# First mixing stage: the steps of the head pairs from the first scores on come half an input unit later

## The chip, the core and the metric

The kernel runs on one core of a Trainium2 chip. A core has several engines that each work through a list of instructions of their own, in order: TensorE (PE in the profile) multiplies matrices and transposes 128x128 tiles, VectorE (DVE) and ScalarE (ACT) work on rows of elements, GpSimd (POOL) does a little elementwise work, and SyncE (SP) issues most transfers from memory. The engines meet through semaphores: an instruction may wait until a counter that others raise has reached a value, and whatever stands behind it in its engine's list waits too. The metric is the device time of one execution in microseconds (us); the median of the runs is compared.

## What is computed

Two blocks of a transformer-like network on 256 positions of 1024 features, all in float32: four feed-forward parts with three mixing parts between them. The change touches only the first mixing part. In the reference it is this:

```python
h = rmsnorm(x, mix_pre_g);  q, k, v, qb, kb, vb = split(h @ w_qkv)
a = gqa_dense(axial_rope(norm(q)), axial_rope(norm(k)), v)    # 8 heads of 64, 2 key/value heads
b = dilated_mixture(rope(qb), rope(kb), vb)                   # 8 heads of 64, windowed patterns
x = x + rmsnorm(concat(a, b) @ w_out, mix_post_g)
```

Each head computes scores q k^T, the exponentials of the scores less the row's maximum, divides by the row's sum, and multiplies with the values. The three dilated patterns of the second kind are folded into one table that is added to the scores.

## The kernel before

To keep float32 accuracy every weight matrix is split in two parts, a rounded "high" and the rest, "low"; each product is made of three passes (`PASSES`). Weights arrive by SyncE in items of 128x2048 numbers (`gu_raw`, two slots). ScalarE writes the high part (`gu_high`, line 1168), VectorE the low part (`gu_low`, line 1808), and only then may TensorE use the item (it waits for `gu_split`). An item's slot may be overwritten by ScalarE when TensorE has finished the item two before it (`wait_used`).

In the first mixing stage (span time 200 to 301 us) TensorE first makes the four pair units 0 to 3, then the input units 4 to 8, each with `project` (line 670: 48 matmuls, 24 for each half, `halves`), and last the output units (`out_unit`, line 793). Between the input units stand the steps of the eight head pairs (`PAIRS`), each a chain that goes from engine to engine:

- TensorE `pair_scores(p)` (line 746) into banks 4 and 5; it waits until the exponentials of pair p-1 are done (`p_ready`, pairs 1 to 4), or its maxima (`max_ready`, from pair 5 on)
- VectorE `pair_max(p)` (lines 2194 and 2197, from pair 4 on 2203 and 2208)
- ScalarE `pair_exps(p)` (line 1494)
- VectorE `pair_normal(p)` (lines 2214 and 2216)
- TensorE `pair_transposes(p)` (line 759), ScalarE `pair_pT_out(p)` (line 1505)
- TensorE `pair_values(p)` (line 777) into one bank, number 3, for pairs 0 to 6. It waits for `o_ready` of the pair before, that is, until ScalarE's `pair_high` (line 1510) and VectorE's `pair_low` (line 2222) have both read that bank.

Beside them run the rotary steps of the queries and keys: `rope_raw` (line 1448) and `rope_in_out` (line 1435) on ScalarE, `rope_turn` (line 2173) and `rope_sum` (line 2182) on VectorE, products on GpSimd (line 2602), `rope_transposes` (line 731) on TensorE. `values_in` (line 1481) takes values out of PSUM.

Nothing sorts this work: the order on each engine is the order in which the calls are written, in three lists by hand, one each for TensorE, ScalarE and VectorE. `next_high(v)` and `next_low(v)` split item v+2 of the stage, in the middle of these lists; `out_high(0, u)` and `out_low(0, u)` split item 11+u.

Short names below: P5a is the first half of input unit 5, P5b the second; S, T and V with a pair's number are the scores, transposes and values of TensorE; M, E and N are a pair's maxima (VectorE), exponentials (ScalarE) and division (VectorE). "Item 8" is the stage's item 8, which input unit 8 uses.

Of the kernel before, what the change touches and what calls it, by code (L numbers as in the profile page):

```python
# [148 lines left out]
def build(nc, a):  # L149
    with ExitStack() as ctx:  # L150
# [245 lines left out]
        def rope_heads(r):  # L396


            return 2 if r == 2 else 4
# [108 lines left out]
        def _(pe):  # L508
# [145 lines left out]
            def project(m, v, feature, halves=range(2)):  # L654

                item = MIX_ITEM[m] + v
                sl = item % 2
                pe.wait_ge(s["gu_split"], item + 1)
                if (m, v) in ((0, 4), (0, 5)):
                    wait_unit(pe, 0, "pair 0")  # L660
                elif v >= 2:
                    wait_unit(pe, m, 0 if v < 4 else v - 2)
                for h in halves:
                    for k in range(KC):
                        for pw_, px in PASSES:
                            wk = gu[pw_][:, sl, k * SEQ:(k + 1) * SEQ]
                            cut_ = slice(h * P, (h + 1) * P)
                            lhsT, rhs = ((wk[:, cut_], hT[px][:, k, :]) if feature
                                         else (hT[px][:, k, cut_], wk))
                            i = nc.tensor.matmul(unit_bank(v)[:, h * SEQ:(h + 1) * SEQ], lhsT, rhs,  # L670
                                                 start=(pw_, px, k) == (0, 0, 0),
                                                 stop=(pw_, px, k) == (1, 0, KC - 1))
                if h == 1:
                    i.then_inc(s["proj_done"], 1)
# [48 lines left out]
            def rope_transposes(k):  # L723

                pe.wait_ge(s["rop_ready"], k + 1)
                if k:
                    pe.wait_ge(s["ropT_evac"], k)
                w = rope_heads(ROPES[k]) * HD
                for c in range(w // P):
                    for t in range(TT):  # L730
                        i = nc.tensor.transpose(bank(2)[:, c * SEQ + t * P:c * SEQ + (t + 1) * P],
                                                rop[:, k % 2, t * w + c * P:t * w + (c + 1) * P], ident[:, :])
                i.then_inc(s["ropT_psum"], 1)

            def pair_scores(p):


                pe.wait_ge(s["ropT_evac"], (2, 2, 3, 3, 5, 5, 7, 7)[p])
                if p:
                    pe.wait_ge(s["p_ready" if p <= PAIRS // 2 else "max_ready"], p)  # L740
                c = p % 4
                for t in range(TT):
                    for e in range(2):
                        half = slice(64 * e, 64 * e + 64)
                        q, k = (qT[0], kTA[half, :]) if p < PAIRS // 2 else (qT[1], kTB[half, c, :])
                        i = nc.tensor.matmul(bank(4 + e)[:, t * SEQ:(t + 1) * SEQ],
                                             q[half, c, t * P:(t + 1) * P], k, start=True, stop=True)
                i.then_inc(s["s_ready"], 1)

            def pair_transposes(p):  # L750

                pe.wait_ge(s["pn_ready"], p + 1)
                if p:
                    pe.wait_ge(s["pt_ready"], p)
                for e in range(2):
                    for kt in range(TT):
                        for t in range(TT):
                            o, f = kt * SEQ + t * P, 2 * SEQ * e + t * SEQ + kt * P
                            i = nc.tensor.transpose(bank(6 + e)[:, o:o + P], pair_probs[:, p % 2, f:f + P],
                                                    ident[:, :])  # L760
                i.then_inc(s["pt_psum"], 1)
# [104 lines left out]
            pair_unit(1, 1, 1, range(4, 8))  # L866
            project(0, 4, False)
            rope_transposes(1)
            pair_scores(0)
            project(0, 5, False)  # L870
            rope_transposes(2)
            pair_scores(1)
            pair_transposes(0)
            project(0, 6, False, (0,))
            rope_transposes(3)
            pair_scores(2)
            pair_values(0)
            pair_transposes(1)
            project(0, 6, False, (1,))
            rope_transposes(4)  # L880
            pair_scores(3)
            pair_values(1)
            pair_transposes(2)
            project(0, 7, False, (0,))
            pair_scores(4)
            pair_values(2)
            pair_transposes(3)
            rope_transposes(5)
            project(0, 7, False, (1,))
            pair_scores(5)  # L890
            pair_values(3)
            pair_transposes(4)
            project(0, 8, False, (0,))
            rope_transposes(6)
            pair_values(4)
            pair_scores(6)
            pair_transposes(5)
            project(0, 8, False, (1,))
            pair_scores(7)
            pair_values(5)  # L900
            pair_transposes(6)
            def pair_out(k):

                return s["o_ready"], k + 1

            wait_unit(pe, 0, 8)
            out_unit(0, 0, 0, range(4), pair_out)
            pe.wait_ge(s["ropT_evac"], 7)
            out_unit(0, 0, 1, range(4), pair_out)
            pair_transposes(7)  # L910
            pair_values(6)
            for t in range(TT):
                out_unit(0, 1, t, (4, 5), pair_out)
            pair_values(7)
# [219 lines left out]
        def _(act):  # L1134
# [304 lines left out]
            def rope_raw(k):  # L1439

                v, r = ROPE_AT[k], ROPES[k]
                if k >= 2:
                    act.wait_ge(s["rop_ready"], k - 1)
                act.wait_ge(s["proj_done"], v + 1)
                w = rope_heads(r) * HD
                src = unit_bank(v).rearrange("p (t n) -> p t n", t=TT)
                for t in range(TT):
                    i = nc.scalar.activation(raw[:, k % 2, t * w:(t + 1) * w], src[:, t, 0:w], ACT.Copy,
                                             scale=st["rinv"][:, t:t + 1])
                i.then_inc(s["raw_ready"], 1)  # L1450
# [61 lines left out]
            def next_high(v):  # L1512

                gu_high(MIX_ITEM[0] + v + 2)
# [18 lines left out]
            step.mark(nc.scalar.activation(st["warm"][:, 0:1], col(COL_HALFPI), ACT.Exp))  # L1533
            step.done(act)
            next_high(4)
            pair_exps(0)
            rope_raw(4)
            values_in(5)
            rope_in_out(2)
            pair_exps(1)  # L1540
            pair_pT_out(0)
            rope_in_out(3)
            next_high(5)
            pair_high(0)
            pair_exps(2)
            pair_pT_out(1)
            rope_raw(5)
            next_high(6)
            rope_in_out(4)
            pair_high(1)  # L1550
            pair_exps(3)
            pair_pT_out(2)
            pair_high(2)
            pair_exps(4)
            pair_pT_out(3)
            rope_in_out(5)
            rope_raw(6)
            next_high(7)
            pair_high(3)
            pair_exps(5)  # L1560
            pair_pT_out(4)
            rope_in_out(6)
            pair_high(4)
            pair_exps(6)
            pair_pT_out(5)
            values_in(8)
            next_high(8)
            pair_high(5)
            pair_exps(7)
            pair_pT_out(6)  # L1570
            pair_pT_out(7)
            out_high(0, 0)
# [229 lines left out]
        def _(dve):  # L1802
# [382 lines left out]
            def next_low(v):  # L2185

                gu_low(MIX_ITEM[0] + v + 2)
# [46 lines left out]
            rope_squares(2)  # L2234
            next_low(3)
            rope_turn(2)
            pair_max(0)
            rope_sum(2)
            rope_turn(3)
            next_low(4)  # L2240
            pair_normal(0)
            pair_max(1)
            rope_sum(3)
            rope_turn(4)
            pair_normal(1)
            rope_sum(4)
            pair_max(2)
            next_low(5)
            pair_low(0)
            pair_normal(2)  # L2250
            pair_max(3)
            next_low(6)
            pair_low(1)
            rope_turn(5)
            rope_sum(5)
            pair_normal(3)
            pair_max(4)
            pair_low(2)
            pair_normal(4)
            pair_max(5)  # L2260
            rope_turn(6)
            rope_sum(6)
            pair_low(3)
            pair_normal(5)
            pair_max(6)
            pair_low(4)
            next_low(7)
            pair_normal(6)
            pair_max(7)
            pair_low(5)  # L2270
            pair_normal(7)
            next_low(8)
            pair_low(6)
            out_low(0, 0)
            pair_low(7)
# [588 lines left out]
```

## Time and profile before

| | us |
|---|---|
| median of 3 runs | 1085.87 (1085.01 to 1086.59) |
| span of the profiled execution | 1083.0 |
| TensorE busy in it | 1067.1 (99%) |
| VectorE busy | 790.6 (73%) |
| ScalarE busy | 589.8 (54%) |
| GpSimd busy | 215.0 (20%) |

The span goes from the first to the last instruction of one profiled execution; 1085.87 - 1083.0 = 2.9 us lie around it. A timeline row is read so: start, duration, engine, line, operation, what it writes and reads, and in brackets how long the engine had been idle before it and who ended that. The recorded duration of an instruction runs some 0.1 us into the start of the next on the same engine, so a step's cost in a row of steps is the distance between starts.

### The profile page before, as it was taken

How to read it: one execution, taken by the hardware profiler on the slowest of the kernel's cores; microseconds unless marked ns; L12 is line 12 of the kernel's file. 1: busy time of each engine (PE TensorE's matmuls, PEld its weight loads, DVE VectorE, ACT ScalarE, POOL GpSimd, SP SyncE). 2: the span in 40 equal slices, each digit the busy share in tenths (PEclk: the TensorE clock that was granted, in tenths of full speed). 3: DMA queues.
4: the chain of work that ended last, by engine and by line, in shares of the span. 5: the costliest groups of instructions: out<-in, count | busy, mean ns of one | idle time of the engine just before them, and what ended most of it. 6: DMA issues, size and time to landing. Idle time of an engine off the chain costs nothing.

```text
span 1083.0 us, 18769 instructions
## 1 busy us (share of the span) xinstructions
PE 1067.1 (99%) x7028; PEld 939.0 (87%) x7028; DVE 790.6 (73%) x1092; ACT 589.8 (54%) x853; POOL 215.0 (20%) x224
## 2 busy tenths in 40 slices
PE   9999999999999999999999999999999999999997
PEld 8888889888788888898998988888899888888886
DVE  5867776897678888766776788777559557777674
ACT  6546444767766445455785644554443565544453
POOL 0006000031069997000000398000000000000001
PEclk9999999999999999999999999999999999999999
DMA  7775455332445656552434754645434235645541
GB/s 260 294 245 203 177 177 206 128 150 79 146 163 187 217 179 228 181 210 95 147 126 156 247 199 175 232 175 177 172 125 161 98 126 183 225 175 181 207 154 39
DMA packets 37025, 189.64 MB, mean 175 GB/s; under 512 B 3824, under 2 KB 4592, under 8 KB 22640
## 3 DMA queue, kind: packets, MB, share of 16 engines
q1 hardware_dynamic: 34528, 181.22, 46.4%
q10 hardware_dynamic: 2160, 6.70, 1.9%
q0 software_dynamic: 288, 1.05, 0.3%
q8 instruction: 33, 0.54, 0.2%
q14 instruction: 16, 0.13, 0.0%
HBM read 187.90 MB, written 1.05 MB: 174 GB/s over the span
## 4 chain that ended last, share of the span: by engine, by line
PE 86%; DVE 6%; ACT 4%; issue 2%; DMA 1%; SPq 0%; DVEq 0%; ACTq 0%
PE ps L558 23%; PE ps L629 19%; PE ps L563 12%; PE ps L670 8%; PE ps L793 6%; PE ps L570 6%; PE ps L590 1%; DMA gu_raw<-in_wgu 1%; DVE gu_low L1808 1%; PE ps L692 1%; PE ps L605 1%; ACT gu_high L1168 1%; PE ps L518 1%; PE ps L710 1%; PE ps L617 1%
## 5 line engine op out<-in xcount | busy, mean ns | idle before, releaser
L558 PE MATMUL ps<-hT,gu_high 128*128 128x512 f32 x1152 | 286.8, 391 | 0.0
L558 PEld LDWEIGHTS ps<-hT,gu_high 128*128 128x128 f32 x1152 | 211.5, 188 | 41.6 <-DVE gu_low L1943 0.4
L1943 DVE TENSOR_TENSOR gu_low<-gu_raw,gu_high 128x2048 fp32r<-128x2048 f32 x83 | 196.0, 2361 | 7.4 <-ACT gu_high L1293 4.3
L563 PEld LDWEIGHTS ps<-hT,gu_low 128*128 128x128 f32 x1152 | 157.2, 190 | 11.2
L1293 ACT ACTIVATE gu_high<-gu_raw 128x2048 fp32r<-128x2048 f32 x84 | 160.4, 1909 | 9.1 <-PE ps L570 8.3
L563 PE MATMUL ps<-hT,gu_low 128*128 128x256 f32 x1152 | 160.6, 282 | 0.0
L1269 ACT ACTIVATE ffn_s<-ffn_s 128x256 f32<-128x256 f32 x88 | 36.8, 418 | 178.5 <-DVE ffn_s L1910 143.4
L1947 DVE TENSOR_TENSOR dn_low<-dn_raw,dn_high 128x1024 fp32r<-128x1024 f32 x84 | 112.1, 1334 | 2.7 <-ACT dn_high L1301 2.7
L1925 DVE TENSOR_TENSOR ffn_s<-ps,ffn_s 128x256 f32<-128x256 f32 x72 | 30.6, 425 | 109.2 <-ACT ffn_s L1281 109.2
L1301 ACT ACTIVATE dn_high<-dn_raw 128x1024 fp32r<-128x1024 f32 x84 | 88.7, 1056 | 35.8 <-PE ps L629 35.8
L1168 ACT ACTIVATE gu_high<-gu_raw 128x2048 fp32r<-128x2048 f32 x37 | 70.8, 1914 | 68.5 <-PE ps L670 35.1
L1808 DVE TENSOR_TENSOR gu_low<-gu_raw,gu_high 128x2048 fp32r<-128x2048 f32 x35 | 81.1, 2318 | 35.8 <-ACT gu_high L1168 35.8
L629 PE MATMUL ps<-dn_high,act_high 128*128 128x512 f32 x320 | 100.2, 394 | 1.2 <-DVE act_low L1935 0.7
L629 PE MATMUL ps<-dn_low,act_high 128*128 128x512 f32 x320 | 99.1, 391 | 0.0
L629 PE MATMUL ps<-dn_high,act_low 128*128 128x512 f32 x320 | 98.9, 390 | 0.0
L629 PEld LDWEIGHTS ps<-dn_low,act_high 128*128 128x128 f32 x320 | 60.1, 188 | 13.4
L629 PEld LDWEIGHTS ps<-dn_high,act_low 128*128 128x128 f32 x320 | 60.1, 188 | 13.1
L670 PE MATMUL ps<-hT,gu_high 128*128 128x256 f32 x384 | 70.2, 285 | 0.0
L570 PE MATMUL ps<-hT,gu_high 128*128 128x256 f32 x384 | 70.0, 284 | 0.0
L1275 ACT ACTIVATE ffn_s<-ps 128x256 f32<-128x256 f32 x72 | 27.3, 379 | 77.3 <-PE ps L563 77.2
L629 PEld LDWEIGHTS ps<-dn_high,act_high 128*128 128x128 f32 x320 | 54.9, 190 | 9.0 <-issue 2.4
L570 PEld LDWEIGHTS ps<-hT,gu_high 128*128 128x128 f32 x384 | 60.3, 192 | 0.6
(336 smaller groups left out, 1865.1 us busy)
## 6 DMA issues: line engine op xcount, KB each, us to landing
gu_raw<-in_wgu SPq DMA_DIRECT2D x126, 1024.0 KB, 4.8
dn_raw<-in_wdn SPq DMA_DIRECT2D x88, 512.0 KB, 5.3
x<-in_x SPq DMA_DIRECT2D x2, 512.0 KB, 5.6
gu_raw<-in_wgu SPq DMA_DIRECT2D x2, 512.0 KB, 6.5
scratch<-in_glu ACTq DMA_DIRECT2D x1, 1024.0 KB, 10.9
scratch<-in_biasM ACTq DMA_DIRECT2D x1, 1024.0 KB, 6.2
s5in<-in_s5in ACTq DMA_DIRECT2D x1, 768.0 KB, 4.3
out_x<-scratch SPq DMA_DIRECT2D x3, 256.0 KB, 2.4
```

Source lines behind the costliest of these rows:

```text
L558: nc.tensor.matmul(out, gu[0][:, sl, o:o + P], hT_both[:, k, :, :].rearrange("p a s -> p (a s)"), start=k == 0, stop=False)
L563: i = nc.tensor.matmul(out[:, 0:SEQ], gu[1][:, sl, o:o + P], hT[0][:, k, :], start=False, stop=k == KC - 1)
L570: i = nc.tensor.matmul(out[:, 0:SEQ], gu[pw_][:, sl, o:o + P], hT[px][:, k, :], start=(pw_, px, k) == (0, 0, 0), stop=(pw_, px, k) == (1, ...
L629: i = nc.tensor.matmul(bank(2 * t + half), act_s[px][:, h, t * P:(t + 1) * P], dn[pw_][:, h, half * 512:half * 512 + 512], start=start and ...
L670: i = nc.tensor.matmul(unit_bank(v)[:, h * SEQ:(h + 1) * SEQ], lhsT, rhs, start=(pw_, px, k) == (0, 0, 0), stop=(pw_, px, k) == (1, 0, KC ...
L793: i = nc.tensor.matmul(out, oT[px][:, k, t * P:(t + 1) * P], both, start=(pw_, px, k) == (0, 0, own) and j % 2 == 0, stop=(pw_, px, k) == ...
L1168: nc.scalar.activation(gu[0][:, g % 2, :], gu_raw[:, g % 2, :], ACT.Copy) \
L1293: nc.scalar.activation(gu[0][:, sl, :], gu_raw[:, sl, :], ACT.Copy) \
L1301: nc.scalar.activation(dn[0][:, 1 - h, :], dn_raw[:, 1 - h, :], ACT.Copy) \
L1808: nc.vector.tensor_tensor(gu[1][:, g % 2, :], gu_raw[:, g % 2, :], gu[0][:, g % 2, :], ALU.subtract).then_inc(s["gu_split"], 1)
L1943: nc.vector.tensor_tensor(gu[1][:, sl, :], gu_raw[:, sl, :], gu[0][:, sl, :], ALU.subtract).then_inc(s["gu_split"], 1)
L1947: nc.vector.tensor_tensor(dn[1][:, 1 - h, :], dn_raw[:, 1 - h, :], dn[0][:, 1 - h, :], ALU.subtract) \
```

## The change

Each of the three lists is written in another order; no instruction is added or removed. On TensorE the units are cut in halves, and each step of a pair stands half a unit further back in the order of the units: S0 came ahead of P5a and now comes ahead of P5b, and so on. V1 stood before P7a and stands behind it, V6 now comes before T7, and the first output unit's first tile comes before V5. The lists of ScalarE and VectorE follow.

```diff
             rope_transposes(1)
+            project(0, 5, False, (0,))
             pair_scores(0)
-            project(0, 5, False)
+            project(0, 5, False, (1,))
             rope_transposes(2)
             pair_scores(1)
+            project(0, 6, False, (0,))
             pair_transposes(0)
-            project(0, 6, False, (0,))
             rope_transposes(3)
             pair_scores(2)
+            project(0, 6, False, (1,))
             pair_values(0)
             pair_transposes(1)
-            project(0, 6, False, (1,))
             rope_transposes(4)
             pair_scores(3)
+            project(0, 7, False, (0,))
             pair_values(1)
             pair_transposes(2)
-            project(0, 7, False, (0,))
             pair_scores(4)
+            project(0, 7, False, (1,))
...
             out_unit(0, 0, 1, range(4), pair_out)
+            pair_values(6)
             pair_transposes(7)
-            pair_values(6)
...
             next_high(4)
+            rope_raw(4)
             pair_exps(0)
-            rope_raw(4)
             values_in(5)
+            next_high(5)
             rope_in_out(2)
...
+            pair_exps(2)
+            rope_raw(5)
+            pair_pT_out(1)
+            rope_in_out(4)
+            next_high(6)
             pair_high(0)
...
             pair_normal(1)
             rope_sum(4)
             pair_max(2)
-            next_low(5)
+            pair_normal(2)
+            rope_turn(5)
+            next_low(6)
+            rope_sum(5)
             pair_low(0)
-            pair_normal(2)
             pair_max(3)
```

In the changed kernel all lines behind TensorE's list stand one further down (1168 is 1169, and so on).

The first place is ScalarE's list around `pair_high(0)`, which writes `dn_high`. Before, from the split of item 7 (line 1168) on:

```order
L1168 ACTIVATE gu_high<-gu_raw 128x2048
L1510 ACTIVATE dn_high<-ps 128x256
L1494 ACTIVATE scratch,stat<-ps,stat 128x256 x4
L1505 ACTIVATE scratch<-ps 128x1024
L1448 ACTIVATE scratch<-ps,small 128x256 x2
L1168 ACTIVATE gu_high<-gu_raw 128x2048
L1435 ACTIVATE scratch<-ps 128x512
```

and now, from E2 on, with the split of item 8 in line 1169:

```order
L1495 ACTIVATE scratch,stat<-ps,stat 128x256 x4
L1449 ACTIVATE scratch<-ps,small 128x256 x2
L1506 ACTIVATE scratch<-ps 128x1024
L1436 ACTIVATE scratch<-ps 128x512
L1169 ACTIVATE gu_high<-gu_raw 128x2048
L1511 ACTIVATE dn_high<-ps 128x256
L1495 ACTIVATE scratch,stat<-ps,stat 128x256 x4
```

`pair_high(0)` stood ahead of E2, behind the split of item 7; it now stands behind E2, three further steps and the split of item 8.

The second place is VectorE's list around `pair_low(0)`, which writes `dn_low`. Before, from M2 on:

```order
L2194 TENSOR_REDUCE stat<-ps 128x2x2
L2197 TENSOR_SCALAR stat<-stat 128x2x2
L1808 TENSOR_TENSOR gu_low<-gu_raw,gu_high 128x2048
L2222 TENSOR_TENSOR dn_low<-ps,dn_high 128x256
L2214 RECIPROCAL stat<-stat 128x2x2
L2216 TENSOR_TENSOR scratch<-scratch,stat 128x1024
L2194 TENSOR_REDUCE stat<-ps 128x2x2
```

and now, from M2 on:

```order
L2195 TENSOR_REDUCE stat<-ps 128x2x2
L2198 TENSOR_SCALAR stat<-stat 128x2x2
L2215 RECIPROCAL stat<-stat 128x2x2
L2217 TENSOR_TENSOR scratch<-scratch,stat 128x1024
L2174 TENSOR_TENSOR scratch<-scratch 128x512
L1809 TENSOR_TENSOR gu_low<-gu_raw,gu_high 128x2048
L2183 TENSOR_TENSOR scratch<-scratch 128x512
L2223 TENSOR_TENSOR dn_low<-ps,dn_high 128x256
L2195 TENSOR_REDUCE stat<-ps 128x2x2
```

The low part of item 7 between M2 and `pair_low(0)` has moved ahead, and N2, `rope_turn(5)`, the low part of item 8 and `rope_sum(5)` now stand there.

The third place is TensorE's list behind the first output unit (line 793): before

```order
L793 MATMUL ps<-gu_high,dn_low 128x512
L793 MATMUL ps<-gu_low,dn_high 128x512
L759 MATMUL ps<-ident,scratch 128x128 x8
L777 MATMUL ps<-scratch 64x256 x4
L793 MATMUL ps<-gu_high,dn_high 128x512
```

and now

```order
L793 MATMUL ps<-gu_high,dn_low 128x512
L793 MATMUL ps<-gu_low,dn_high 128x512
L777 MATMUL ps<-scratch 64x256 x4
L759 MATMUL ps<-ident,scratch 128x128 x8
L793 MATMUL ps<-gu_high,dn_high 128x512
```

V6 (line 777) has moved from behind T7 (line 759) to ahead of it.

## Rows read from the trace of the kernel before

**Rows 1.** The page, part 1: busy time, share of the span and instructions of each engine.

```profile
PE 1067.1 (99%) x7028; PEld 939.0 (87%) x7028; DVE 790.6 (73%) x1092; ACT 589.8 (54%) x853; POOL 215.0 (20%) x224
```

**Rows 2.** TensorE's timeline, 228 to 238 us: where it stood idle.

```profile
228.08 1.14 PE L746 MATMUL ps<-scratch 64*128 64x256 f32 x8 [0.69 <-ACT scratch L1435]
...
237.15 1.09 PE L759 MATMUL ps<-ident,scratch 128*128 128x128 f32 x8 [0.49 <-DVE scratch L2216]
```

**Rows 3.** The chain that ended last, in order of time, 238 to 244 us.

```profile
238.25 2.87 PE ps L670 x24
241.12 0.44 PE ps L731 x4
241.55 1.06 PE ps L746 x8
242.62 1.01 PE ps L777 x8
243.63 1.02 PE ps L759 x8
```

**Rows 4.** VectorE's timeline: item 5's low part, steps of the pairs, the last `pair_low`.

```profile
225.96 2.28 DVE L1808 TENSOR_TENSOR gu_low<-gu_raw,gu_high 128x2048 fp32r<-128x2048 f32 x1
...
232.60 2.83 DVE L1808 TENSOR_TENSOR gu_low<-gu_raw,gu_high 128x2048 fp32r<-128x2048 f32 x1
...
246.62 0.17 DVE L2214 RECIPROCAL stat<-stat 128x4 f32<-128x4 f32 x1
246.82 1.23 DVE L2216 TENSOR_TENSOR scratch<-scratch,stat 128x1024 f32<-128x1024 f32 x1
249.07 1.23 DVE L2194 TENSOR_REDUCE stat<-ps 128x4 f32<-128x1024 f32 x1 [1.02 <-PE ps L746]
250.33 0.17 DVE L2197 TENSOR_SCALAR stat<-stat 128x4 f32<-128x4 f32 x1
250.40 2.29 DVE L1808 TENSOR_TENSOR gu_low<-gu_raw,gu_high 128x2048 fp32r<-128x2048 f32 x1
252.61 0.42 DVE L2222 TENSOR_TENSOR dn_low<-ps,dn_high 128x256 fp32r<-128x256 f32 x1
...
253.66 0.69 DVE L2182 TENSOR_TENSOR scratch<-scratch 128x512 f32<-128x512 f32 x1
...
287.89 0.42 DVE L2222 TENSOR_TENSOR dn_low<-ps,dn_high 128x256 fp32r<-128x256 f32 x1
```

**Rows 5.** ScalarE's timeline, 247 to 254 us, without its accumulator reads.

```profile
247.62 0.84 ACT L1448 ACTIVATE scratch<-ps,small 128x256 f32<-128x256 f32 x2 [0.56 <-PE ps L670]
248.34 1.91 ACT L1168 ACTIVATE gu_high<-gu_raw 128x2048 fp32r<-128x2048 f32 x1
250.15 0.60 ACT L1435 ACTIVATE scratch<-ps 128x512 f32<-128x512 f32 x1
250.62 0.39 ACT L1510 ACTIVATE dn_high<-ps 128x256 fp32r<-128x256 f32 x1
250.89 0.49 ACT L1494 ACTIVATE scratch<-ps,stat 128x256 f32<-128x256 f32 x1
...
252.68 1.07 ACT L1505 ACTIVATE scratch<-ps 128x1024 f32<-128x1024 f32 x1
```

**Rows 6.** GpSimd's timeline: the rotary products of two steps (x2 each).

```profile
229.16 1.95 POOL L2602 TENSOR_TENSOR scratch<-scratch 128x256 f32<-128x256 f32 x2 [5.61 <-DVE scratch L2162]
232.03 3.98 POOL L2602 TENSOR_TENSOR scratch<-scratch 128x256 f32<-128x256 f32 x2 [0.93 <-DVE scratch L2182]
```

**Rows 7.** The same chain behind T7, 282 to 286 us.

```profile
282.18 1.01 PE ps L777 x8
283.20 2.94 PE ps L793 x12
```

**Rows 8.** Windows at the end of the span: length, busy us (instructions), granted clock, DMA.

```profile
1075.00:1080.00 5.00, 0.56 (x3) 0.13 (x1) 3.55 (x7) 2.69 (x7) 3.25 (x2) 1.00 0.16 61
1080.00:1083.00 3.00, 0.00 (x0) 0.00 (x0) 0.00 (x0) 0.00 (x0) 0.00 (x0) 0.53 0.66 247
```

More of the change, by code:

```diff
@@ L888, in _ @@
             rope_transposes(5)
-            project(0, 7, False, (1,))
             pair_scores(5)
+            project(0, 8, False, (0,))
+            rope_transposes(6)
             pair_values(3)
             pair_transposes(4)
-            project(0, 8, False, (0,))
-            rope_transposes(6)
+            pair_scores(6)
+            project(0, 8, False, (1,))
             pair_values(4)
-            pair_scores(6)
             pair_transposes(5)
-            project(0, 8, False, (1,))
             pair_scores(7)
-            pair_values(5)
-            pair_transposes(6)
             def pair_out(k):
@@ L907, in _ @@
             out_unit(0, 0, 0, range(4), pair_out)
+            pair_values(5)
+            pair_transposes(6)
             pe.wait_ge(s["ropT_evac"], 7)
             out_unit(0, 0, 1, range(4), pair_out)
+            pair_values(6)
             pair_transposes(7)
-            pair_values(6)
             for t in range(TT):
@@ L1542, in _ @@
             rope_in_out(3)
-            next_high(5)
-            pair_high(0)
[L1545 to L1549, printed above, removed]
+            pair_exps(2)
[3 more added lines that the diff above has]
+            next_high(6)
+            pair_high(0)
+            pair_exps(3)
             pair_high(1)
-            pair_exps(3)
             pair_pT_out(2)
+            pair_exps(4)
+            rope_raw(6)
             pair_high(2)
-            pair_exps(4)
             pair_pT_out(3)
             rope_in_out(5)
-            rope_raw(6)
             next_high(7)
+            pair_exps(5)
+            rope_in_out(6)
             pair_high(3)
-            pair_exps(5)
             pair_pT_out(4)
-            rope_in_out(6)
+            pair_exps(6)
+            values_in(8)
             pair_high(4)
-            pair_exps(6)
             pair_pT_out(5)
-            values_in(8)
             next_high(8)
+            pair_exps(7)
             pair_high(5)
-            pair_exps(7)
             pair_pT_out(6)
@@ L2236, in _ @@
             rope_turn(2)
+            rope_sum(2)
             pair_max(0)
-            rope_sum(2)
             rope_turn(3)
@@ L2241, in _ @@
             pair_normal(0)
+            rope_sum(3)
             pair_max(1)
-            rope_sum(3)
             rope_turn(4)
+            next_low(5)
             pair_normal(1)
@@ L2247, in _ @@
             pair_max(2)
-            next_low(5)
+            pair_normal(2)
+            rope_turn(5)
+            next_low(6)
+            rope_sum(5)
             pair_low(0)
-            pair_normal(2)
             pair_max(3)
-            next_low(6)
+            pair_normal(3)
             pair_low(1)
-            rope_turn(5)
-            rope_sum(5)
-            pair_normal(3)
             pair_max(4)
+            pair_normal(4)
+            rope_turn(6)
             pair_low(2)
-            pair_normal(4)
+            rope_sum(6)
             pair_max(5)
-            rope_turn(6)
-            rope_sum(6)
+            next_low(7)
+            pair_normal(5)
             pair_low(3)
-            pair_normal(5)
             pair_max(6)
+            pair_normal(6)
             pair_low(4)
-            next_low(7)
-            pair_normal(6)
             pair_max(7)
+            next_low(8)
+            pair_normal(7)
             pair_low(5)
-            pair_normal(7)
-            next_low(8)
             pair_low(6)
```

## The prediction, made before the changed kernel was run

> **What bounds the kernel now.** I read the page first: TensorE is busy for 99% of the span [rows 1]. A step on another engine costs nothing while TensorE has work, and each microsecond that TensorE stands idle is lost. TensorE's timeline comes next, from the second rotary transpose (227 us) to the last output unit (301 us). It shows two idle pieces: 0.69 us ahead of S0 and 0.49 us ahead of T0 [rows 2]. From there on the chain that ended last is TensorE's own list, step behind step [rows 3]. So the change can win at most 0.69 + 0.49 = 1.2 us, 0.1% of the span, since it takes no instruction away. What it can lose is set by the chains between the engines, which had slack behind 238 us and get another order.
>
> **The prices.** TensorE: a half unit 2.87, rotary transposes 0.44, scores 1.06, values 1.01, transposes 1.02 [rows 3]. VectorE: a low part 2.2 to the next step and 2.3 to its signal (recorded 2.29, with the next step 2.21 behind its start); maxima from 249.07 to 250.33 + 0.17 = 250.50, 1.4; division from 246.62 to 246.82 + 1.23 = 248.05, 1.4; rotary turn or sum 0.6 between starts (recorded 0.69), `pair_low` 0.4 [rows 4]. ScalarE, by distances between starts: `rope_raw` 0.7, a high part 1.8, `rope_in_out` 0.5, `pair_high` 0.3, four exponentials 250.89 to 252.68, 1.8 and 0.1 more to the signal; the copy of the transposes 1.0 [rows 5].
>
> **Wait 1, P5a.** P5a now stands where S0 stood. TensorE is free at 228.08 - 0.69 = 227.4 [rows 2]. S0 waited there for the rotary queries; P5a needs the low part of item 5, which ends at 225.96 + 2.28 = 228.2 [rows 4], and its place in VectorE's list has not moved. P5a starts at 228.3: wait 0.9. The old wait is not taken away; it gets 0.2 longer with another name.
>
> **Wait 2, S1.** S0 starts at 228.3 + 2.87 = 231.2, ends at 232.2. M0 starts at 232.3 and ends at 233.7, E0 ends 1.9 later, 235.7 (the `rope_raw` now ahead of E0 is done by then: GpSimd's products for its slot end at 229.16 + 1.95 = 231.1 [rows 6], the sum 0.7 later, and it takes 0.7 itself). TensorE is ready for S1 at 232.2 + 2.87 + 0.44 = 235.5. Before, the whole of unit 5 stood between S0 and S1; now one half. Wait 0.2, S1 at 235.7.
>
> **Wait 3, S2.** VectorE goes on from M0 at 233.7: turn 0.6, low part of item 6 2.2, N0 1.4, sum 0.6, M1 1.4: 239.9. N0 and the sum now stand ahead of M1. E1 ends at 241.8, S2 can start at 241.9. TensorE: 235.7 + 1.06 + 2.87 + 1.02 + 0.44 = 241.1. Wait 0.8. P6a needs item 6's low part, ready at 236.6, when S1 ends at 236.8: no wait. T0 comes at 239.6, N0 is done at 237.9: the old wait of 0.49 ahead of T0 is gone, covered by P6a.
>
> **Wait 4, V1, the main one.** V1 overwrites bank 3 and needs `pair_low(0)`. The chain to it, from M1's end at 239.9: VectorE turn 0.6, low part of item 7 2.2, N1 1.4, sum 0.6, M2 1.4: 246.1. ScalarE E2 1.9, `rope_raw(5)` 0.7, copy 1.0, `rope_in_out` 0.5, high part of item 8 1.8: 252.0. VectorE can't begin the low part of item 8 before, and behind it stand `rope_sum(5)` and then `pair_low(0)`: 2.2 + 0.6 + 0.4 = 3.2, 255.2. TensorE comes to V1 at 241.9 + 1.06 (S2) + 2.87 (P6b) + 1.01 (V0) + 1.02 (T1) + 0.44 + 1.06 (S3) + 2.87 (P7a) = 252.2. Wait 3.0. `pair_high(0)` needs V0, which is over at 246.8, so it is the order of ScalarE's and VectorE's lists that holds it, not TensorE: it is queued behind E2, three steps and a high part. P7a, now ahead of V1, is no cover for it: it has been counted.
>
> **Wait 5, S4.** M3 stands in VectorE's list behind `pair_low(0)`: 255.2 + 1.4 = 256.6, E3 ends at 258.5. TensorE comes to S4, which needs E3, at 255.2 + 1.01 + 1.02 = 257.2. Wait 1.3.
>
> **Then cover again.** From S4 on each S has at least a half unit and two steps of a pair behind it (2.87 + 1.01 + 1.02 = 4.9 us) while S waits, from S5 on, for the maxima of the pair before alone (1.4 in the dense form; the form with the table has no row here, and even twice that is covered). The other moves of items lie under this and cost 0, as long as that slack of some 2 us holds.
>
> **Wait 6, the last pair.** From T7's end at 282.18 [rows 7] to the end of `pair_low(7)` at 287.89 + 0.42 = 288.31 [rows 4] there are 6.1 us: copy, high part of item 11, `pair_high(6)`, low part of item 11, `pair_low(7)`, none of which moves. Before, TensorE had V6 1.01, four pieces of output 2.94, V7 1.01 and two pieces 2.94 / 2 = 1.47 between [rows 7], 6.4 us, just enough. V6 now stands ahead of T7: 5.4 us are left against 6.1 and the signal. Wait 0.8.
>
> **The sum.** 0.9 + 0.2 + 0.8 + 3.0 + 1.3 + 0.8 = 7.0 us of waits, less the 1.2 us that were there: 5.8 us more. One price is not settled: GpSimd's products of one step took 3.98 us in place of 1.95 [rows 6], and the low part begun beside them 2.83 in place of 2.28 [rows 4]. Now the same products begin with M0, near 232, and the low part of item 6 at 234.3. If they still meet, 0.55 is added to M1 and S2 with it: 6.3. If not, 5.8. I take 6.0, since half of the products' long time reaches past 234.3. Everything behind the stage is relative to TensorE's last output unit and shifts whole: 1083.0 + 6.0 = 1089.0 of span, and with the 2.9 us around it **1091.9**.
>
> The Trainium skill, GPSIMD Engine Reference, section Specifications, says that GpSimd shares its SBUF interfaces with VectorE and that the contention comes with VectorE instructions in a two-port mode or with two SBUF inputs. The maxima read PSUM, so by that rule the products would be over sooner and the sum 5.8; rows 6 and 4 agree with the collision itself, and no row shows the products beside the maxima.
>
> **Rivals.**
> - *The halves do cover.* What the order is for: each chain gets half a unit more, both old waits go, nothing replaces them. 1085.87 - 1.2 = 1084.7, not slower. For it: behind 238 us the old chain has no step of another engine in it, V1 had no wait at all [rows 3]. It decides at V1: the chain from M1 to `pair_low(0)` must be 3 us shorter than its 15.3 us, and M3 with it. Against it: its pieces are queued work with recorded durations, not waits. It could only be if `pair_high(0)` did not stand where the list of ScalarE puts it, which the rows of the order exclude. Chance 0.06, of it 0.02 for faster by over 0.2%.
> - *The chains are a little quicker.* Steps on VectorE and ScalarE run 5% under the rows. Each S-to-S and the V1 chain then shrink, waits 2 and 3 nearly go and wait 4 falls by 0.8: some 3.7 us more, 1089.6. Chance 0.08.
> - *The clock falls.* TensorE stands idle 3.0 us, works 2.0 and stands 1.3. In the old trace the granted clock stays 1.00 through the window with 0.56 us of work in 5 and is 0.53 in the next [rows 8], so the lower level, 1.2 GHz, comes behind an idle stretch longer than this one. If it came here, V1, T2 and P7b (1.01 + 1.02 + 2.87 = 4.9 us) would take up to double: 2 to 5 us on top, 1094 to 1097. Chance 0.08.
> - *More waits in a row.* The slack behind S4 is less than I count and S3, S6 or a T waits too: 7.5 to 8.5 us, up to 1094.4. Chance 0.08.
>
> The Trainium skill, TensorE: Matmul & The Clock Gate, section Why this matters for your kernels, warns of gaps of idle between bursts of matmuls, after which the clock goes back to the half rate. By that rule the third rival would be likelier than I put it; the trace's own long idle stretch, with the clock still full in its first part, speaks for the lower chance.
>
> **How the numbers follow.** Forecast 0.70, rivals 0.06, 0.08, 0.08, 0.08. The range runs from the quick chains (1089.2, a little under 1089.6) to the many waits (1094.5); it leaves out the first rival and the clock. A measurement of this kernel can tell about 0.2% (2.2 us) from no change, so the bounds are 1083.7 and 1088.0: faster 0.02, within 0.05, slower 0.93.
>
> **What would show it.** Right: TensorE's timeline after has an idle piece of some 3 us ahead of V1 (line 778), released by `dn_low`, at 252 us; one of about 1 us ahead of S4, released by exponentials; one under 1 us in the output unit behind V7; no idle piece ahead of T0; and P5a waits for `gu_low` where S0 waited. The first part of the span up to 227 us is as before. Wrong: V1 starts within 0.5 us of P7a's end; or the granted clock is below 1.00 between 250 and 270 us; or the time is lost behind 301 us.

## The result, and the profile after

The changed kernel takes 1094.55 us (median of 4 runs, 1093.11 to 1095.16) against 1086.23 us (4 runs, 1085.01 to 1086.80): a ratio of 1.0080, 95% interval 1.0068 to 1.0092. It is slower, as forecast, by 8.3 us where 6.0 was forecast, and 1094.55 lies 0.05 us above the range's end of 1094.5. A second set of the same two kernels gave 1093.16 against 1085.59, 7.6 us; that time lies inside the range. So on which side of the bound the time falls is scatter; that more than 6.0 us are lost shows in the length of the stage, below.

The profiled execution of the changed kernel has a span of 1092.5 us; its own time was 1094.26, so 1.8 us lie around a span. The page of after, busy time (compare [rows 1]): TensorE does the same work in a longer span.

```profile
PE 1070.8 (98%) x7028; PEld 940.7 (86%) x7028; DVE 790.3 (72%) x1092; ACT 590.3 (54%) x853; POOL 213.8 (20%) x224
```

TensorE's timeline of after, the rows behind an idle stretch in the first mixing stage (start, duration, what; in brackets the idle time before it and who ended it). They answer to [rows 2].

```profile
229.91 0.51 PE L670 MATMUL ps<-gu_high,hT 128*128 128x256 f32 x2 [1.09 <-DVE gu_low L1809]
...
244.04 1.14 PE L746 MATMUL ps<-scratch 64*128 64x256 f32 x8 [0.83 <-ACT scratch L1495]
...
257.32 1.18 PE L777 MATMUL ps<-scratch 128*64 128x256 f32 x8 [2.48 <-DVE dn_low L2223]
...
260.62 1.60 PE L746 MATMUL ps<-scratch 64*128 64x256 f32 x8 [0.22 <-ACT scratch L1495]
...
297.67 0.47 PE L793 MATMUL ps<-gu_high,dn_high 128*128 128x512 f32 x1 [0.90 <-DVE dn_low L2223]
```

There were two idle stretches, 1.2 us in all; now there are five, 5.5 us. In the order of the rows: P5a for item 5's low part; S2 for E1; V1 for `pair_low(0)`; S4 for E3; the output unit for `pair_low(7)`. These are the places that the prediction named, with the releasers that it named, and T0 waits no more.

One number for the stage serves all runs: from the start of the second rotary transposes to the start of the next part's first transposes. Before it is 300.89 - 226.80 = **74.1 us**, after 309.99 - 228.21 = **81.8 us**. So 7.7 us are lost in the stage. TensorE's timeline of after at the two ends:

```profile
228.21 0.60 PE L731 MATMUL ps<-ident,scratch 128*128 128x128 f32 x4
...
309.99 1.16 PE L518 MATMUL ps<-ident,x 128*128 128x128 f32 x8
```

The windows of after, where the stage's clock is not full (length, busy us of TensorE, its weight loads, VectorE, ScalarE, GpSimd, granted clock, DMA share, GB/s):

```profile
256.00:258.00 2.00, 0.68 (x7) 0.57 (x8) 2.00 (x4) 0.00 (x0) 0.00 (x0) 1.00 0.18 25
258.00:260.00 2.00, 2.00 (x12) 1.57 (x8) 0.48 (x2) 1.45 (x7) 0.00 (x0) 0.55 0.93 348
260.00:262.00 2.00, 1.78 (x10) 1.11 (x8) 1.45 (x3) 1.67 (x5) 0.00 (x0) 0.60 0.38 152
262.00:264.00 2.00, 2.00 (x18) 1.85 (x16) 1.90 (x10) 0.04 (x1) 0.00 (x0) 1.00 0.00 0
```

The third rival came too, in small: behind V1's wait the granted clock fell to half, the lower of its two levels (1.2 GHz), for some 3 us. T2 and S4 ran in that stretch; TensorE's timeline shows T2 of after and then T2 of before, the same eight transposes.

```profile
258.43 1.97 PE L759 MATMUL ps<-ident,scratch 128*128 128x128 f32 x8
```

```profile
249.97 1.09 PE L759 MATMUL ps<-ident,scratch 128*128 128x128 f32 x8
```

### The profile page after: what moved, and what is told of

Its sections match the earlier page's. It is cut to its first block, busy times and chain, and to the rows that moved or that the text cites. A ratio compares the mean times of both kernels' runs of the same rounds, so it can differ in the third digit from the quotient of the medians.

```text
span 1092.5 us, 18770 instructions
## 1 busy us (share of the span) xinstructions
PE 1070.8 (98%) x7028; PEld 940.7 (86%) x7028; DVE 790.3 (72%) x1092; ACT 590.3 (54%) x853; POOL 213.8 (20%) x224
## 3 DMA queue, kind: packets, MB, share of 16 engines
q0 software_dynamic: 288, 1.05, 0.3%
HBM read 187.90 MB, written 1.05 MB: 173 GB/s over the span
## 4 chain that ended last, share of the span: by engine, by line
PE 85%; DVE 7%; ACT 4%; issue 2%; DMA 1%; SPq 0%; DVEq 0%; ACTq 0%
PE ps L558 22%; PE ps L629 19%; PE ps L563 12%; PE ps L670 7%; PE ps L570 6%; PE ps L793 6%; PE ps L590 2%; DVE gu_low L1809 2%; DMA gu_raw<-in_wgu 1%; ACT gu_high L1169 1%; PE ps L692 1%; PE ps L518 1%; PE ps L605 1%; PE ps L710 1%; PE ps L617 1%
```

## The experiments

In each the stage's length is what is compared. It was 81.8 and 81.7 us in two profiles of the changed kernel, though single waits ahead of an edit also moved by up to 0.25 us from one profile to the next; the time of a run repeats only within 1 to 2 us. "Price" below is the distance between the starts of two neighbours in TensorE's list.

**1. The changed kernel again (e1_again).**

> The changed kernel once more. Measure of all runs: the stage's length on TensorE, from the start of the second rotary transposes (line 731 or 732, behind unit 4) to the start of the next part's first transposes (line 518); before 300.89 - 226.80 = 74.1 us, changed 309.99 - 228.21 = 81.8 us. Theory (all of the loss is in the stage): 81.8 within 0.3 again, with the clock at half speed for some 3 us behind V1's wait; the 1.4 us by which the changed kernel's profile was later already at the stage's start is scatter of the start, and is another number here. Rival: that offset comes with the change; then it is 1.4 again.

Measured: stage 81.7, time 1.0065 times before (1.0048 to 1.0082), the same waits to 0.01 us (V1 2.49, S2 0.83, the output unit 0.90), clock at half speed again from 257 to 260 us. Its stage starts at 227.0 instead of 228.2. The loss of 7.6 to 7.7 us is the stage's; the 1.4 us by which after's profile was late at the stage's start is scatter.

**2. `pair_low(0)` alone ahead of item 8's split (e2_low0).** On ScalarE and VectorE:

```diff
             pair_exps(2)
+            pair_high(0)
             rope_raw(5)
             pair_pT_out(1)
             rope_in_out(4)
             next_high(6)
-            pair_high(0)
...
             pair_normal(2)
+            pair_low(0)
             rope_turn(5)
             next_low(6)
             rope_sum(5)
-            pair_low(0)
             pair_max(3)
```

> Changed kernel, pair_high(0) straight behind E2 and pair_low(0) straight behind N2, ahead of the split of item 8. Theory (queues): V1's wait of 2.5 us goes, but M3 is still behind the low part of item 8 and rope_sum(5), so E3 ends near 260 and the wait moves to S4, some 3.4 us instead of 0.2 and the slow T2; stage 80.5 to 81.3. Rival (V1's bank is the loss): stage 78.7 or less, S4 waits under 1.5 us.

Measured: stage 82.8; ratio 1.0082 (1.0057 to 1.0107). V1 starts 3.07 us after P7a, with no wait; the wait is at S4. TensorE's timeline of this run:

```profile
258.65 2.08 PE L746 MATMUL ps<-scratch 64*128 64x256 f32 x8 [3.68 <-ACT scratch L1495]
```

3.68 us of idle where 3.4 were expected, and not a microsecond won: M3 is still queued behind the low part of item 8, and S4 needs M3. What was not expected is 1.5 us more on top: the granted clock is at half for some 3 us as in after, but here that stretch falls on S4, which takes 2.0 instead of 1.06, and on the next half unit, which takes 3.68 instead of 3.07. Here nothing covers it.

```profile
258.00:260.00 2.00, 1.35 (x6) 1.32 (x8) 1.43 (x3) 1.69 (x5) 0.00 (x0) 0.67 0.56 225
260.00:262.00 2.00, 2.00 (x10) 1.35 (x8) 1.54 (x8) 0.00 (x0) 0.00 (x0) 0.50 0.00 0
```

(Windows of this run, columns as above.)

**3. M3 too ahead of item 8's split (e3_low0_max3).** As 2, and on VectorE `pair_max(3)` behind `pair_low(0)`, ahead of `rope_turn(5)`.

> As e2_low0, and M3 too stands ahead of the low part of item 8. Theory (queues): V1 and S4 wait for nothing, the clock stays at 1.00: 2.6 (V1) + 1.3 (T2 and S4's wait) + 0.5 (S4 at half clock) less, stage 77.4 within 0.4, about 4.3 us under the changed kernel. Rival: another late step takes their place, stage over 79.

Measured: stage 78.2; time 1.0028 times before (1.0018 to 1.0038), 1089.3 us. Neither V1 nor S4 waits, the clock is 1.00. 3.6 us are won where 4.3 were expected, and 78.2 lies outside the expected 77.4 within 0.4; the difference is a wait that was hidden behind the others, S6 for the rotary keys' copy, in TensorE's timeline of this run:

```profile
269.96 1.13 PE L746 MATMUL ps<-scratch 64*128 64x256 f32 x8 [0.60 <-ACT scratch L1436]
```

So the order of two steps against one split of an item makes V1's and S4's waits, and both have to move. (That M3 alone would not do is argued, not run: V1 would still wait for `pair_low(0)`.)

**4. Matmuls in the wait (e4_fill).** On TensorE:

```diff
             project(0, 7, False, (0,))
+            fill(20, 1)
             pair_values(1)
```

> Changed kernel with 20 matmuls of 128x128 on the identity ahead of V1, into a part of a bank that is not read, so that TensorE works through 2.2 us of its wait of 2.5. Theory (the clock fell because TensorE stood idle): granted clock 1.00 all through, T2 takes 1.1 instead of 2.0, S4 1.1 instead of 1.5; since T2's loss was covered by S4's wait for E3, only S4's 0.5 us is won: stage 81.3, S4 waits 1.1 us. Rival (the fall has another cause): clock 0.5 for some 3 us again, stage 81.8 or more.

Measured: stage 82.0, ratio 1.0065 (1.0047 to 1.0083). The clock is 1.00 all through and S4 takes 1.07; but the 20 took 4.6 us, twice what I had reckoned, and pushed V1 1.9 us back, so that this run says nothing on what the fall costs.

**5. The same with nine (e9_fill9).** `fill(9, 1)` in place of `fill(20, 1)`.

> As e4_fill, with 9 matmuls instead of 20: those 20 took 4.6 us and outlasted the wait, 9 should take 2.1. Theory (the clock falls behind an idle stretch of 2.5 us, and costs only the part that S4's wait does not cover): clock 1.00, V1 starts 5.6 us after P7a's start as in the changed kernel, T2 takes 1.0, S4 waits 1.1 us for E3 and takes 1.06; stage 81.2. Rival (the clock's fall costs what T2 and S4 lose together): 80.3.

Measured: stage 81.7, ratio 1.0073 (1.0058 to 1.0089). The filler took 2.2 us of the wait and left 0.46; V1 starts 5.61 us after P7a as it did (5.62), the clock stays at 1.00. The windows of this run:

```profile
250.00:260.00 10.00, 8.35 (x70) 7.16 (x68) 6.57 (x9) 5.64 (x14) 2.08 (x2) 1.00 0.30 107
260.00:270.00 10.00, 10.00 (x82) 8.46 (x79) 7.42 (x23) 6.88 (x15) 2.41 (x2) 1.00 0.01 2
```

and TensorE's timeline:

```profile
259.52 1.13 PE L746 MATMUL ps<-scratch 64*128 64x256 f32 x8 [1.19 <-ACT scratch L1496]
...
273.09 1.13 PE L746 MATMUL ps<-scratch 64*128 64x256 f32 x8 [0.28 <-ACT scratch L1437]
```

S4 now waits 1.19 us for E3, visible where T2's slow run had hidden it, and takes 1.06. That is 0.5 us less up to P7b. But S6 now waits 0.28 for the rotary keys, which it did not when TensorE was 0.5 us later, and 0.1 us are left of the gain (81.78 to 81.68, no more than the scatter of 81.78 and 81.66). In this kernel, at this place, the fall costs nothing that can be measured, since other waits stand behind it. That the filler kept the clock up is likely but not shown: in experiment 6 the clock stays full without one. There S4's wait for E3 is 1.19 us and S6's 0.28 too, so these two waits come with a full clock and not with the filler.

**6. V6 behind T7 again (e5_tail).**

```diff
-            pair_values(6)
             pair_transposes(7)
+            pair_values(6)
```

> Changed kernel with V6 behind T7 again, as before. Theory (cover of T7's chain): the idle 0.9 us in the output unit behind V7 goes, stage 80.9 (81.8 less 0.9). Rival: V6's place does not matter, 81.8, because the chain from T7 starts 1 us earlier only.

Measured: stage 80.4; ratio 1.0063 (1.0047 to 1.0078). The idle 0.90 us at the output unit is gone. 1.4 us are won where 0.9 were expected. The part from S7 on makes 1.1 of it (between experiments 3 and 8 the same edit makes 1.0), and P5a's wait, which stands ahead of the edit, was 0.25 shorter by chance (0.84 against 1.09). V1 waited 2.47 us again, but this time the clock did not fall: windows of this run.

```profile
256.00:258.00 2.00, 0.02 (x2) 0.05 (x2) 2.00 (x4) 0.00 (x0) 0.00 (x0) 1.00 0.05 10
258.00:260.00 2.00, 2.00 (x16) 1.38 (x16) 1.13 (x2) 0.80 (x3) 0.00 (x0) 1.00 0.75 238
260.00:262.00 2.00, 0.81 (x7) 0.75 (x8) 0.80 (x2) 2.00 (x8) 0.00 (x0) 1.00 0.69 281
```

**7. One part of the change at a time.** TensorE's list of the change with the two other lists of before (e6_pe_only), and TensorE's of before with the two others of the change (e7_lists_only).

> TensorE's list of the change, ScalarE's and VectorE's of before. There pair_low(0) stands behind the low part of item 7, S4 needs E3, and M3 stands ahead of the split of item 8. Theory (the order on ScalarE and VectorE makes V1's wait): V1 waits under 1 us and the stage is 77 to 80. Rival (TensorE's half unit alone is the loss): 81 or more.

> TensorE's list of before, ScalarE's and VectorE's of the change. V1 comes 3 us earlier in TensorE's list (ahead of P7a) than in the change, its pair_low(0) is where the change puts it. Theory: V1 waits 5 us or more, the clock falls, stage 80 to 83. Rival (the lists matter only with the halves): under 77.

Measured: stages 87.7 and 88.4, ratios 1.0147 and 1.0122, each far worse than the change as a whole. The expected sums failed for both, the single waits did not. The 87.7 lies where the first expectation's rival has it (81 or more), but that rival, the half unit alone as the loss, does not follow: the same list of TensorE comes to 77.1 in experiment 8. With the old lists V1 waits for nothing, as expected, but P6a, S3, S4, RT6, S6 and the first output unit now wait for steps that the old lists hold for later. With the new lists and the old TensorE V1 waits 6.0 us, and the clock falls as expected: it is 0.50 from 254 to 260 us. It falls a second time in that run, behind an idle stretch of only 1.9 us (0.63 from 280 to 282 us and 0.52 from 282 to 284), while with the old lists it stays at 1.00 behind 2.8 us of idle ahead of S6. The waits view of the two, TensorE's:

```profile
PE ps L746 <- ACT scratch L1436: 2.8, 1, 2.8
...
PE ps L731 <- DVE scratch L2183: 1.8, 1, 1.8
...
PE ps L793 <- ACT scratch L1482: 2.0, 1, 2.0
```

```profile
PE ps L777 <- DVE dn_low L2222: 6.0, 1, 6.0
...
PE ps L777 <- ACT scratch L1505: 4.0, 3, 1.9
```

The three lists are one order; changing a part of it is no half of the change.

**8. The changed kernel mended (e8_fixed).** The edits of experiments 3 and 6 together, and no other.

> Changed kernel with pair_high(0), pair_low(0) and M3 moved as in e3_low0_max3 and V6 behind T7. Left are P5a's wait (1.1), S1's 0.1 and S2's 0.9. With TensorE's steps at the same price in every order, the stage is 74.1 - 0.6 (T0's wait) + 0.6 (P5a against S0) + 1.0 = 75.1 us. If the order of TensorE's steps has a price of its own (transposes ahead of a unit give way after 0.85 us, scores after 1.06, values or scores behind transposes after 1.02), some 0.17 us for each of 7 or 8 blocks, it is 76.4. In time: slower than before by 1.0 or 2.3 us, both hard to tell from no change.

Measured: stage 77.1; 1088.6 us, 1.0023 times before (1.0014 to 1.0032). Against 74.1 of before the waits add up to 1.75 us: P5a 0.58 more than S0 had, S1 0.14, S2 0.92, S6 0.67, less 0.56 at T0. That leaves 1.28 us without any idle time in the profile. With flat prices there would be none; by the second expectation 1.3. (The stage as a whole is 0.7 over that expectation's 76.4: it left out S6's wait, which experiment 3 had shown.) So the order of TensorE's steps has a price. Before, each block of steps ended in transposes, with a unit behind them; now it mostly ends in scores. TensorE's timeline of this run, starts of a scores step and of the unit behind it:

```profile
255.59 1.13 PE L746 MATMUL ps<-scratch 64*128 64x256 f32 x8
256.65 0.50 PE L670 MATMUL ps<-gu_high,hT 128*128 128x256 f32 x2
```

1.06 us, where a unit follows transposes after 0.85: before, T2 at 249.97 and the unit behind it.

```profile
250.81 0.48 PE L670 MATMUL ps<-gu_high,hT 128*128 128x256 f32 x2
```

The transposes are only half of it: added up over the stage, they cost 0.6 us more than before. The input half units cost 0.5 more and the first output unit 0.2, because a unit's own length depends on what stands behind it too. TensorE's timeline of before shows a half unit with rotary transposes behind it, 2.95 us, and that of the changed kernel one with values behind it, 3.05 us.

```profile
238.00 0.48 PE L670 MATMUL ps<-gu_high,hT 128*128 128x256 f32 x2
...
240.95 0.60 PE L731 MATMUL ps<-ident,scratch 128*128 128x128 f32 x4
```

```profile
245.11 0.50 PE L670 MATMUL ps<-gu_high,hT 128*128 128x256 f32 x2
...
248.16 1.08 PE L777 MATMUL ps<-scratch 128*64 128x256 f32 x8
```

**9. Two blocks with the transposes last (e10_t_last).** As 8, with

```diff
             pair_values(2)
-            pair_transposes(3)
             rope_transposes(5)
             pair_scores(5)
+            pair_transposes(3)
...
             pair_values(4)
-            pair_transposes(5)
             pair_scores(7)
+            pair_transposes(5)
```

> As e8_fixed (stage 77.12), with T3 and T5 moved to the end of their blocks, straight ahead of a unit. Theory (TensorE's order has a price: a unit's first matmul follows transposes after 0.85 us, scores after 1.06): 0.15 to 0.2 less for each of the two blocks, stage 76.7 to 76.85, no new wait. Rival (prices are flat and the 1.3 us left over in e8_fixed lie elsewhere): 77.1.

Measured: stage 76.9, 0.19 less; ratio 1.0022 (1.0012 to 1.0031). The block of T5 gives 0.19 us, as expected; the block of T3, where rotary transposes and scores stand between, gives less, 0.05 (0.10 without the 0.05 by which S5 stands further from the rotary transposes). S6 waits 0.07 longer. So the sum stays a little short of the expected one.

**10. Before, with the values last in three blocks (e11_v_last).** On TensorE, three times as here:

```diff
-            pair_values(0)
             pair_transposes(1)
+            pair_values(0)
```

> The kernel before (stage 74.1) with V behind T in three blocks (V0 and T1, V1 and T2, V3 and T4), so that values and not transposes stand ahead of the next half unit. All three have their inputs in time. Theory (order has a price): 0.15 to 0.2 more for each, stage 74.55 to 74.7, no wait. Rival (flat): 74.1.

Measured: stage 74.8, 0.74 more than before; 0.20 of it is a longer wait of T0, which has nothing to do with the edit, and 0.54 are left for three blocks, 0.18 each, as expected (74.6 without T0's longer wait). No new wait. Ratio 1.0007 (0.9998 to 1.0016): too small for a measurement of time, plain in the stage.

**11. Before, with T0 behind P6a (e12_t0).** The one move of the change that covers a wait and starts none:

```diff
-            pair_transposes(0)
             project(0, 6, False, (0,))
+            pair_transposes(0)
```

> The kernel before with one move: T0 behind P6a instead of ahead of it. T0's wait of 0.49 us is covered by P6a, and T0 no longer stands ahead of a unit, which costs 0.1 to 0.2. Stage 73.7 to 73.85, time within 0.1% of before. Rival: V0's chain is late then, and V0 waits; over 74.1.

Measured: stage 73.6, 0.5 less than before, no wait ahead of T0 or V0. That is a little better than expected: T0's new place costs 0.05 us and not 0.1 to 0.2. T0, straight behind a unit, gives way to the rotary transposes after 0.87, where T1 and T3, straight behind values, take 0.93 in after. Ratio 0.9993 (0.9984 to 1.0002): no difference that a measurement of this kernel can tell, but it is the half microsecond that the change had to give.

## Where the prediction was right and where it was wrong

The forecast's direction, its places, its releasers and the order of their sizes held; the size was 6.0 for 7.7 in the stage. Term by term, measured as prices in after against before:

| term | forecast, us | measured, us |
|---|---|---|
| 1: P5a for S0 | 0.9 less 0.69 | 1.34 less 0.75 |
| 2: S1 | 0.2 | 0.14 |
| 3: S2 | 0.8 | 0.90 |
| T0's old wait | -0.49 | -0.56 |
| 4: V1 | 3.0 | 2.57 |
| 5: from V1's start to P7b | 1.3 | 1.73 |
| 6: output unit behind V7 | 0.8 | 1.05 |
| order of TensorE's steps (what is left) | 0 | 1.27 |
| sum | 5.8 | 7.7 |

- **The failed step is the list of prices.** I took TensorE's prices from the chain view [rows 3] and held them to be the same in every order, so that only waits could cost. Nothing in my sum stood for the order itself. The old trace had the rows that would have told it: transposes ahead of a unit give way after 0.85, scores after 1.06; a half unit gives way to rotary transposes after 2.95, to scores after 3.04. Experiments 8, 9 and 10 show 0.10 to 0.19 us for each block. The 1.27 us of after are 0.5 in the transposes, 0.4 in the input half units (unit 5 whole took 5.86, its halves 3.06 and 2.98) and 0.3 in the first output unit, which is now cut in more pieces. Half a microsecond of it hides in V1's wait, so with this term the forecast would have been 5.8 + 1.3 - 0.5 = 6.6. Most of the other 1.1 us are terms that were sized too low: P5a 0.4, the way from V1's start to P7b 0.4, in which S4 ran at half clock, and the last pair 0.25.
- **Wait 1** was 0.4 larger. In part this is the flat price again: the rotary transposes give way to a unit after 0.36 us, where I had TensorE free 0.6 behind their start. The other 0.2: the low part of item 5 ends 1.64 us behind that start and not 1.44 as before.
- **Wait 4** was in the right place for the right reason, shown by experiments 2 and 3. The chain of the other engines from M1's end to `pair_low(0)`'s end took 257.18 - 241.94 = 15.2 us against my 15.3, which also refutes the rival of quicker chains. The wait was 0.4 smaller because TensorE took 257.32 - 2.48 - 244.04 = 10.8 us from S2's start to V1's place where I had 10.3: the dearer order, half a microsecond of it hidden here.
- **Wait 5** is E3's, shown by experiments 2 and 3 and by 1.19 us in experiment 5. In after itself it shows as 0.22 us of idle only, since T2 ran at half clock in front of it. The rest of the 1.73 is S4 at half clock (1.53 us to its neighbour instead of 1.07) and 0.1 at V1.
- **"Then cover again"** was wrong in one place: S6 has no slack. RT6's copy stands behind E5 in ScalarE's list. In after it does not show, because TensorE is late enough; in experiments 3, 5, 6, 8 and 9 it costs 0.35 to 0.75 us.
- **The collision on GpSimd** did not happen. Its products beside M0 took 1.42 us (before 3.98, [rows 6]) and the low part behind them 2.29, so the 5.8 was the right end of that choice, as the Trainium skill's rule in GPSIMD Engine Reference, section Specifications, had it. The prediction says that no row shows the products beside the maxima; those shown do not, but the old trace has M0 beside the products of 229.16 us, which took 1.95 and not 3.98. Its row of VectorE's timeline of before, and then GpSimd's and VectorE's timelines of after:

```profile
229.72 1.22 DVE L2194 TENSOR_REDUCE stat<-ps 128x4 f32<-128x1024 f32 x1
```

```profile
233.64 1.42 POOL L2603 TENSOR_TENSOR scratch<-scratch 128x256 f32<-128x256 f32 x2 [0.93 <-DVE scratch L2183]
```

```profile
236.10 2.29 DVE L1809 TENSOR_TENSOR gu_low<-gu_raw,gu_high 128x2048 fp32r<-128x2048 f32 x1
```

- **The clock** was given as a rival with 0.08, by the argument that the trace kept the full clock through a longer idle stretch at its end [rows 8]. One stretch shows how late the clock can fall, not how early; here it fell behind 2.5 us of idle in two profiles of three, behind 1.9 us in the second kernel of experiment 7, and not behind 2.8 us in the first. So the length of the idle stretch alone does not tell whether it falls. The warning of the Trainium skill, TensorE: Matmul & The Clock Gate, section Why this matters for your kernels, that the clock goes back to the half rate after gaps of idle between bursts of matmuls, agrees with these falls. My price for it, 2 to 5 us on top, did not hold either: 0.0 to 0.1 in after (experiments 5 and 6), 1.5 in experiment 2, where no other wait covered it.
- **The first rival**, that the halves cover, is refuted for the change as it stands. Mended in two places (experiment 8) it comes within 0.2% of before, still slower: what is left are the waits of P5a, S2 and S6 and the price of the order. P5a's wait was foreseen: a unit that is put ahead needs its weights that much earlier.
- **The rival of quicker chains** has a slip in its sum: 5.8 less 0.2, 0.8 and 0.8 is 4.0 us, not 3.7.
- **The range** ended at 1094.5, made of the sum's own uncertainties. It had nothing for terms that were missing from the sum.

What stays open: why VectorE reaches the low part of item 5 earlier against TensorE in some profiles of the same list (it ends 1.39 us behind the rotary transposes' start in experiment 6 and 1.54 in experiment 2, 1.64 in after, and P5a's wait follows it: 0.84, 1.00, 1.09), whether P5a's and S2's waits could be taken out, which no run tried, and why the dearer order is dearer. The rows show the distances between starts, not what fills them.

## What to carry to other kernels

Before delaying a chain's steps on one engine, follow the chain's hand-overs on the others and look for a long step of other work, here the split of an item, that now stands ahead of a short one; half a unit more on TensorE, 3 us, did not cover a queue in which the split of item 8 alone takes 1.8 us on ScalarE and 2.2 us behind it on VectorE. A single step moved out of such a queue only hands the wait to the next step of the chain that is still in it. And when steps are put in another order, read the distances between starts for each pair of neighbours, not one price per step.

## What the runs showed of the hardware

- The distance from a step's start to its neighbour's depends on the neighbour: eight 128x128 transposes give way to a unit's matmuls after 0.85 us, to rotary transposes after 0.93 (0.87 where the eight stand straight behind a unit), to scores or values after 0.96 to 1.02. A half unit of 24 matmuls gives way to transposes after 2.94 to 2.98, to scores or values after 3.04 to 3.07. Scores give way to a unit after 1.06 and values after 1.01, no sooner than to transposes.
- The granted clock fell to half behind an idle stretch of 2.5 us in two profiles of the changed kernel, and stayed full behind the same stretch in experiment 6. In experiment 7 it fell behind 1.9 us in one kernel and stayed full behind 2.8 us in the other. It did not fall in either run in which fillers took up the stretch. Once fallen it was full again after some 3 us of work.
- The filler's matmuls of two 128x128 float32 tiles took 0.23 us each (20 in 4.6 us), almost twice a transpose of the same size (8 in 1.02 us); the profile has two records for each of them and one for a transpose.
